# A one-layer streaming encoder step on one core: tail turns moved, keys in two places, norms moved, squares in PSUM

## The reference

```python
h = rmsnorm(x, g_mix); proj = h @ w_in            # 1024 x 2560
a, gate, q, k, v = split(proj)                    # 512 each, 8 heads x 64
u = a * sigmoid(gate)
c = causal_dwconv(concat(past_conv, u), w_dw) + b_dw      # 31 taps a channel
c = silu(layernorm(c, g_cn, b_cn)) @ w_pw
q, k = rmsnorm per head; z = q.k/8, masked s < t
A[t,s] = sigmoid(z[t,s]) * prod_{s<j<t} (1 - sigmoid(z[t,j]))
o = A @ v
x = x + concat(c, o) @ w_out
x = x + relu(rmsnorm(x, g_ff) @ w_ff1)**2 @ w_ff2         # 4096 wide
```

## Time and profile before

| | |
|---|---|
| time, median of 3 | 3094.45 us (3091.27 to 3097.13) |
| the profiled execution | 3089.33 us, span 3087.5 us |
| busy | PE 2774.3 us (90%), DVE 1719.1 (56%), ACT 1008.2 (33%), POOL 753.0 (24%) |
| DMA | 616.19 MB, mean 200 GB/s |
| mean granted PE clock | 0.955 of full |

### The profile page before, as it was taken

The page is one execution under the profiler, slowest core; times in us unless marked ns, Lnnn a source line. Parts: engine busy times, 40 slices in busy tenths (PEclk is TensorE's granted clock), DMA queues, the critical chain, the costliest instruction groups (busy, mean ns, idle before and its releaser), DMA issues. The chain is left out here.

```text
span 3087.5 us, 37298 instructions
## 1 busy us (share of the span) xinstructions
PE 2774.3 (90%) x13936; PEld 2304.8 (75%) x13936; DVE 1719.1 (56%) x2617; ACT 1008.2 (33%) x2017; POOL 753.0 (24%) x622
## 2 busy tenths in 40 slices
PE   5679766798999989899999989899999999999999
PEld 4556555677778777778888878677778777888887
DVE  4686663655667246646777436753778862322222
ACT  4222432234555112124554221222555540211110
POOL 4431332444555102102222002200333320000000
PEclk9789878899999999899999999899999999999999
DMA  8277457567676855656554653674444347344342
GB/s 308 102 259 268 145 183 256 218 242 259 235 258 230 309 202 190 216 180 245 185 181 161 251 205 134 201 253 180 152 161 158 110 163 287 154 173 155 149 179 86
DMA packets 262047, 616.19 MB, mean 200 GB/s; under 512 B 23217, under 2 KB 159409, under 8 KB 213741
## 3 DMA queue, kind: packets, MB, share of 16 engines
q1 hardware_dynamic: 261869, 613.80, 55.8%
HBM read 444.79 MB, written 168.94 MB: 199 GB/s over the span
## 5 line engine op out<-in xcount | busy, mean ns | idle before, releaser
L1081 POOL TENSOR_TENSOR beta<-beta,stay 128x512 f32<-128x512 f32 (+3 forms) x328 | 324.5, 992 | 769.6 <-DVE stay L1722 769.6
L1862 PE MATMUL ps<-h2T_hi,w_s 128*128 128x512 f32 (+1 forms) x1280 | 467.5, 365 | 15.3 <-ACT kqT L1252 7.9
L2152 PE MATMUL ps<-w_s,hid_hi 128*128 128x512 f32 (+1 forms) x1088 | 437.0, 402 | 20.9 <-DVE hid_lo L1796 20.9
L1863 PE MATMUL ps<-h2T_lo,w_s 128*128 128x512 f32 (+1 forms) x1280 | 455.4, 356 | 0.0
L1864 PE MATMUL ps<-h2T_hi,w_s 128*128 128x512 f32 (+1 forms) x1280 | 455.3, 356 | 0.0
L2153 PE MATMUL ps<-w_s,hid_lo 128*128 128x512 f32 (+1 forms) x1088 | 426.1, 392 | 0.0
L2154 PE MATMUL ps<-w_s,hid_hi 128*128 128x512 f32 (+1 forms) x1088 | 425.8, 391 | 0.0
L1352 ACT ACTIVATE stay<-ps 128x512 f32<-128x512 f32 (+3 forms) x328 | 173.5, 529 | 495.9 <-DVE ps L1710 272.5
L994 POOL TENSOR_TENSOR w_s<-w_raw,w_s 128x1024 fp32r<-128x1024 f32 x94 | 244.7, 2623 | 327.1 <-ACT w_s L1138 327.1
L1791 DVE TENSOR_TENSOR resid<-ps,resid 128x512 f32<-128x512 f32 x256 | 176.1, 688 | 258.2 <-PE ps L2154 257.7
L1526 DVE SCALAR_TENSOR_TENSOR cacc<-uT,vecs,cacc 128x512 f32<-128x512 f32 (+1 forms) x360 | 288.5, 857 | 1.5
(11 more groups left out here) (195 smaller groups left out, 4963.0 us busy)
## 6 DMA issues: line engine op xcount, KB each, us to landing
w_s<-w_scratch SPq DMA_DIRECT2D x282, 1024.0 KB, 7.7
w_scratch<-w_s SPq DMA_DIRECT2D x94, 1024.0 KB, 8.0
w_raw<-in_w_ff SPq DMA_DIRECT2D x64, 512.0 KB, 5.0
a_k<-k_scratch SPq DMA_DIRECT2D x80, 256.0 KB, 4.1
a_v<-v_scratch SPq DMA_DIRECT2D x80, 256.0 KB, 3.9
a_q<-q_scratch SPq DMA_DIRECT2D x64, 256.0 KB, 4.7
w_raw<-in_w_in SPq DMA_DIRECT2D x20, 512.0 KB, 7.4
mix_scratch<-ohl SPq DMA_DIRECT2D x66, 128.0 KB, 2.8
```

Source lines behind the costliest of these rows:

```text
L1081: nc.gpsimd.tensor_tensor(v[0:q.r, 0:n], v[0:q.r, 0:n], stay[q.z % 3][0:q.r, 1:n + 1], ALU.mult).then_inc(s_a, 1)
L1862: nc.tensor.matmul(out, w[0], x[0], start=start, stop=False)
L1863: nc.tensor.matmul(out, w[0], x[1], start=False, stop=False)
L2152: nc.tensor.matmul(o, hid_hi[x][:, k, q0:q0 + r], wh[:, c0:c0 + BANK], start=k == 0, stop=False)
```

## The change

- Tail of `kvq(c)`, c = 0, 2, 3: the last two query tiles are turned, copied and stored in slots of the next stage (`TAIL_TURN`: slots 2 and 6 of `front()`, 1 and 3 of a window). The turns use banks 3 and 7, the events the three banks 4 to 6, and PE waits for the last gate (`ag_u`) ahead of the first event.
- Chunk 0's attention: heads take turns in two places for keys and values, so SP loads two heads ahead; `att_past(0)` is 58 in place of 78, so the 41 steps lie in slots 31 to 57 and the loads for `out(0)` are issued at slot 58. Chunk 1's taps in `front()` are moved: 8 in slots 31 to 57 in place of 24, and 47 from slot 58 on in place of 31.
- Chunk 1's input norm goes from `ag(0)` to `kvq(0)` (squares and roots to the second half of `ag(0)`, scaling to its end, turns after events 0 to 3, in banks 1 and 2). The loads of `xsecond` move from the start into `ag(0)`.
- `xin` has four buffers; tiles 2 and 3 are loaded at the end of the window ahead of `out`.
- Feed forward: ACT writes Relu and then Square into the bank itself; DVE's product and `hid_f` go. ff2 results 0 and 1 are interleaved, so that the matmuls of k = 3 come after 18 others in place of 9.
- The transposes for the conv state in the last window go from slot 1 to slot 6.

```diff
 def att_past(c):
-    return 78 if c == 0 else 116
+    return 58 if c == 0 else 116
...
-        hid_f = [place("hid_f0", [P, 4, CHUNK], F32, o_hid + 8 * KIB),
-                 place("hid_f1", [P, 4, TMAX], F32, o_a + 8 * KIB + 4 * TMAX * 4)]
...
-        xin = place("xin", [P, 2, D], F32, o_a + 36 * KIB)
+        xin = [place(f"xin{i}", [P, D], F32, o) for i, o in enumerate(
+            (o_a + 36 * KIB, o_a + 40 * KIB, o_hid + 8 * KIB, o_hid + 12 * KIB))]
...
+        def norm_bank(which, c):
+            return 4 if which else 1 if c == 1 else 6
+
+        def kv_place(c, head):
+
+            return head % 2 * BANK if c == 0 else 0
...
+        KVQ_BANK, KVQ_BANKS, TURNED = 4, 3, (3, 7)
+
+        TAIL_TURN = [(2, 6), (1, 3), (1, 3), (1, 3)]
+
+        def tail_turn(c, slot, later):
+
+            n = len(kvq_events(c))
+            return [n - 2 + k for k in range(2) if c != 1 and TAIL_TURN[c][k] + later == slot]
...
-                due = 0 if t < a else min(n, 5 * (t - a + 1) // 4) if t < 31 else n * 4 // 13 + (n - n * 4 // 13) * (t - 30) // 58
+                due = 0 if t < a else 5 * (t - a + 1) // 4 if t < 31 else 25 + (t - 30) // 3 if t < 58 else 34 + 3 * (t - 57) // 2
...
-                if i >= 2:
-                    sp.wait_ge(n_tp[0], 2 * (4 * c + i - 1))
-                sp.dma_start(xin[0:r, i % 2, :], src).then_inc(x_in[i % 2], 16)
+                if i >= 4:
+                    sp.wait_ge(n_tp[0], 2 * (4 * c + i - 3))
+                elif i >= 2:
+                    sp.wait_ge(f2_ps, 8 * FFE * (c - 1))
+                sp.dma_start(xin[i % 4][0:r, :], src).then_inc(x_in[i % 4], 16)
...
+                    if c == 0 and a < 4:
+                        sp.dma_start(xsecond[:, a, :], x_prompt[0, CHUNK + P * a:CHUNK + P * (a + 1), :]).then_inc(xf_in[a], 16)
...
             def load_keys(c, head, s):
-                sp.dma_start(a_k[:, s * BANK:(s + 1) * BANK].bitcast(F32),
+                at = s * BANK + kv_place(c, head)
...
+                if c == 0:
+                    load_keys(0, 1, 0)
+                    load_values(0, 1, 0)
...
+                    following = q.head + (1 if c else 2)
+                    if q.p == 1 and q.ends and following < NH:
                         sp.wait_ge(z_ps, q.z + 1)
-                        load_keys(c, q.head + 1, q.a0 // BANK)
+                        load_keys(c, following, q.a0 // BANK)
...
+                        for late in tail_turn(n, s, 2):
+                            store_turned(n, late)
...
+                if 0 < n < NC - 1:
+                    for i in range(2, 4):
+                        load_x(n + 1, i)
...
-                    if c == 0 and a == 0:
-                        for i in range(4):
-                            norm_squares(0, 1, i)
-                        act.wait_ge(cache_out, 32)
-                    if c == 0 and a in (3, 5, 7):
-                        norm_hi(0, 1, a // 2 - 1)
+                    if c == 0 and a >= 4:
+                        norm_squares(0, 1, a - 4)
...
-                        nc.scalar.activation(hid_f[x][:, j, s0:s0 + w], bank, ACT.Relu).then_inc(f_rel, 1)
+                        nc.scalar.activation(bank, bank, ACT.Relu).then_inc(f_rel, 1)
+                        act.wait_ge(f_rel, f + 1)
+                        nc.scalar.activation(bank, bank, ACT.Square).then_inc(f_sq, 1)
...
-                    if c == 0:
-                        if m < CB - 1:
-                            norm_scale(0, 1, m)
-                        if m == CB - 2:
-                            norm_scale(0, 1, 3)
                     if m < CB - 1:
                         if m == 0:
                             dve.wait_ge(vec_ok, 2)
                             dve.wait_ge(cache_out, 32)
                         dve.wait_ge(ag_u, 4 * c + (m + 1) * ns)
                         convolve(c, range(EARLY * m, EARLY * (m + 1)))
-                    if c == 0 and m:
-                        norm_lo(0, 1, m - 1)
+                    if c == 0 and m == CB - 2:
+                        norm_scale(0, 1, 0)
                 if c == 0:
-                    norm_lo(0, 1, 3)
+                    for i in range(1, 4):
+                        norm_scale(0, 1, i)
...
+                    if c == 0 and 1 <= s <= 4:
+                        norm_lo(0, 1, s - 1)
...
-                        dve.wait_ge(f_rel, f + 1)
-                        nc.vector.scalar_tensor_tensor(out=bank, in0=bank, scalar=0.0, in1=hid_f[x][:, j, s0:s0 + w],
-                                                       op0=ALU.max, op1=ALU.mult).then_inc(f_sq, 1)
-                    if pos >= 8:
-                        ev = pos - 8
+                    results = [] if pos < 9 else [0, 1] if pos == 9 else [pos - 8]
+                    for ev in results:
...
+            def turn_both(c, s):
+                sec, i, m = kvq_events(c)[s]
+                if sec != "v":
+                    for q in range(2):
+                        if m:
+                            pe.wait_ge(kqT_ok, 2 * (8 * c + m) + q - 1)
+                        turn_packed(c, s, q, TURNED[q])
+
             def kvq(c):
                 evs = kvq_events(c)
                 if c:
                     pe.wait_ge(n_lo[1], 2 * (4 * (c - 1) + len(tiles(c - 1))))
-                else:
-                    pe.wait_ge(n_lo[0], 16)
-                for s in range(len(evs) + 2):
-                    if s < len(evs):
-                        if s >= 4:
-                            pe.wait_ge(kvq_cp, 12 * c + s - 3)
-                        project(c, s, 4 + s % 4, range(KD))
+                for s in range(len(evs)):
+                    if s >= KVQ_BANKS:
+                        pe.wait_ge(kvq_cp, 12 * c + s - KVQ_BANKS + 1)
+                    if s == 0:
+                        pe.wait_ge(ag_u, 4 * c + 4 * len(splits(c)))
+                    project(c, s, KVQ_BANK + s % KVQ_BANKS, range(KD))
+                    if c == 0 and s < 4:
+                        norm_turn(0, 1, s)
                     if s >= 2:
-                        sec, i, m = evs[s - 2]
-                        if sec != "v":
-                            for q in range(2):
-                                if m:
-                                    pe.wait_ge(kqT_ok, 2 * (8 * c + m) + q - 1)
-                                elif q == 0:
-                                    pe.wait_ge(ag_u, 4 * c + 4 * len(splits(c)))
-                                turn_packed(c, s - 2, q, q)
+                        turn_both(c, s - 2)
...
-                pe.wait_ge(kqT_ok, 16)
-                pe.wait_ge(kvq_cp, 12)
                 for t in range(FRONT):
+                    for late in tail_turn(0, t, 0):
+                        turn_both(0, late)
+                    if t == ln0(0):
+                        pe.wait_ge(kqT_ok, 16)
+                        pe.wait_ge(kvq_cp, 12)
...
+            def second(c, e, ev, ks):
+
+                i, hf = ev // 2, ev % 2
+                q0, r = tiles(c)[i]
+                nt, ns, x = len(tiles(c)), len(splits(c)), c // (NC - 1)
+                if 0 in ks:
+                    if ev < 3:
+                        pe.wait_ge(f_lo, 4 * FFE * c + 4 * ns * (e + 1) - (2 - ev))
+                    else:
+                        pe.wait_ge(f2_add, 8 * FFE * c + 2 * nt * e + ev - 2)
+                o = ps[0:r, ff_bank(c, e, 4 * ns + ev), :]
+                for k in ks:
+                    if ev < 2:
+                        pe.wait_ge(f_lo, 4 * FFE * c + 4 * ns * e + (k + 1) * ns)
+                    wh, wl = slab("f2", c, 4 * e + k)
+                    c0 = hf * BANK
+                    nc.tensor.matmul(o, hid_hi[x][:, k, q0:q0 + r], wh[:, c0:c0 + BANK], start=k == 0, stop=False)
+                    nc.tensor.matmul(o, hid_lo[x][:, k, q0:q0 + r], wh[:, c0:c0 + BANK], start=False, stop=False)
+                    ins = nc.tensor.matmul(o, hid_hi[x][:, k, q0:q0 + r], wl[:, c0:c0 + BANK], start=False, stop=k == 3)
+                if 3 in ks:
+                    ins.then_inc(f2_ps, 1)
...
+                        for late in tail_turn(n, s, 0):
+                            turn_both(n, late)
+                        if s == TAIL_TURN[n][1] + 2:
+                            pe.wait_ge(kqT_ok, 2 * (8 * n + 2 * len(tiles(n))))
+                            pe.wait_ge(kvq_cp, 12 * n + 3 * len(tiles(n)))
...
+                        if ev == 0:
+                            second(c, e, 0, range(3))
+                            second(c, e, 1, range(1))
+                        elif ev == 1:
+                            second(c, e, 1, range(1, 3))
+                            second(c, e, 0, range(3, 4))
+                            second(c, e, 1, range(3, 4))
                         else:
-                            pe.wait_ge(f2_add, 8 * FFE * c + 2 * nt * e + ev - 2)
-                        o = ps[0:r, ff_bank(c, e, 4 * ns + ev), :]
-                        for k in range(4):
```

(9 more changed lines are left out.)

93 lines of the change are left out of this document (47 added, 46 removed).

## The result

The changed kernel takes 3022.20 us (median of 4 runs, 3019.73 to 3026.41); before, beside it, 3094.52 (3091.27 to 3097.13). The ratio is 0.9773, 95% interval 0.9761 to 0.9784: 70 us faster by the ratio, 72 by the medians. The forecast was 2981, range 2940 to 3035. So the sign and the range held, and the time is 41 us above the forecast. The profiled execution took 3021.44 us, with a span of 3019.6: 68 of the 112 us in the sum came.

What follows compares the result with a forecast made beforehand. PE was taken as the bound in the feed-forward windows, so only its idle time and slow clock could be won. Terms 27 + 28 + 10 + 15 + 15 + 17 = 112 us off 3089 gave 2977, predicted median 2981, range 2940 to 3035.

Steps and rivals of the forecast that it cites:

- A: Start up to chunk 0's layer norm: chunk 1's norm leaves ag(0), last turns covered by front() slots; -27 us.
- The page weighed in A: Skill page: DVE with one SBUF input isn't blocked by GpSimd, so eight norm_lo cost 5.5 us, not 17.
- B: Attention in front(), slots 31 to 79: key waits go, steps take 2.7 us; -28 us.
- C: End of front(): mix loads issued at slot 58 shorten the 17.41 us wait before out(0); -10 us.
- D: Tails of kvq(2) and kvq(3): waits for the last turned tiles go; -15 us.
- E: Input tiles of chunks 2 and 3: third tile's waits of 9.64 and 5.68 us shrink by earlier loads; -15 us.
- F: Feed forward: most of the 20.9 us of waits for hid_lo go; -17 us.
- R1: Start and front() held by transfers and DVE: gain 45 to 80 us, about 3025 us; chance 0.16.
- the forecast's own: Band of the main forecast for the whole kernel: -80 to -140 us; chance 0.64.
- R3: ACT becomes the bound of the windows, slower, about 3205 us; chance 0.04 with anything slower.

Runs made afterwards that it cites:

- `pw_late`: Changed kernel with the two casts of the pw slabs 5 slots later on ACT, behind the squares of chunk 0's layer norm: 3024.01 us, ratio 0.9780.
- `half_reload`: Changed kernel with work left out: reloads of chunk 1's 20 projection slabs fetch only the high half, 0.5 MB in place of 1 MB: 3010.69 us, ratio 0.9733.
- `tails_x`: Changed kernel with last two turned tiles of chunks 2 and 3 turned at slot 0, their later input tiles loaded late as before: 3039.40 us, ratio 0.9820.
- `ff_order`: Changed kernel with Square kept on ACT and only the interleaving of the first two ff2 results taken back: 3042.72 us, ratio 0.9839.
- `ff_old`: Changed kernel with the old feed forward: Relu into SBUF, product on DVE, 9 matmuls ahead of group 3's first user: 3042.62 us, ratio 0.9842.
- `mix_later`: Changed kernel with chunk 0's 4 MB of mix loads issued at slot 71 of front() in place of slot 58: 3016.42 us, ratio 0.9754.
- `old_pace`: Changed kernel with chunk 0's attention over slots 31 to 77, mix loads at slot 78 and the old tap schedule; two key places kept: 3010.91 us, ratio 0.9734.
- `taps_even`: Changed kernel with mix loads at slot 71 and the old, even tap schedule in front(); attention stays packed: 3014.73 us, ratio 0.9757.

## Why the prediction was right and where it was wrong

- **A, forecast 27, measured 10.** Up to 96 us it came as worked out: event 0 at 95.4 (forecast 96), waits of 9.8 and 3.3 to 3.8 us. Three steps failed behind it. The first is "these three events take 3.3 + 1.1 + 1.1 + 5.4 = 11 us": the waits were right, but the turns and matmuls were priced at the full clock, and events 2 and 3 took 14.4 and 14.0 us at a granted clock of 0.74. At event 5 (163.2 before, 153.3 now) 9.9 us were left, where 16 were forecast. The second is "PE's last waits of this stage, 12 us of those of L1933 in the earlier trace rows, are covered by slots of `front()`, where PE meets DVE again at slot 10": it is not DVE that PE meets there. PE's first matmul of the layer norm came at 230.31 (245.95 before; the prediction read 248), a gain of 15.6: the slots covered 5.7 us and not 11. DVE's last tap ended at 226.6, 9 us ahead of before, and DVE stood idle. What came last was the copy and the store of the last turned tile, moved into `front()` with its turn; `pw_late` showed that its copy can come 9 us earlier for nothing, `half_reload` that the bytes beside it count. The third is that the norm itself was put at nothing: from its first matmul to pw it took 25.4 us before and takes 30.8 now, with the wait for that store in it. The forecast counted PE and DVE in this stretch and not its DMA, although the row for it could have been asked for: 0.64 is the mean over the 93 us of the earlier trace rows, and the last 22 of these read, in the kernel before:

```profile
200.00:222.00 22.00, 9.10 (x40) 7.36 (x40) 21.05 (x30) 6.06 (x12) 13.02 (x10) 0.82 1.00 357
```

- **The page weighed in A** held: `norm_lo`, one input in SBUF and one in PSUM, took 1.27 us for two beside POOL's gain product (DVE, at 112.14), 0.64 each. By the row of `packed` it would have been 2.1. `packed`, with both inputs in SBUF, took 1.35 us beside the same kind of POOL instruction (at 122.87), and taps with theirs in SBUF 1.98 each beside the splits (the four at 433.83). The Trainium skill (SBUF — State Buffer, Who interferes with whom) has it so. The term failed elsewhere.
- **B, forecast 28, and C, 10; measured 14.7 together.** The waits on keys are gone, and the attention of 41 steps runs from 287.0 to 399.8, 2.75 us a step (forecast 2.7). That the size fits is partly luck: 8.2 of these 112.8 us are the wait behind the `ohl` store, which no term had. The step that failed is "The 22 slots after them are 22 x 1.36 = 30 and six turns, 36 us". With the 3 us taken off B and C's rest of 17 the forecast comes to 56 us from there to `out(0)`; it took 78.6. These slots were priced by PE alone. They hold the v stores behind the mix loads, the four splits on POOL, the taps and the q tiles' chain. C's own wait did shrink (3.72, forecast 6 to 8), but what the 4 MB cost had moved ahead, to the v stores and the wait at 454.5. That the key places at the old pace bring 28.5 us, the size of B, is chance: B took that from a sum in which the attention was packed, and packing with mix loads and taps costs 13.8.
- **D and E, forecast 15 + 15.** Taking them back costs 15 to 20 us (`tails_x`), in which one wait of each tail is missing. Behind `out(0)` 42.9 us were won; less the 18.4 of the interleaving, at most 24.5 are left for both, so the pair was put at least 5 us too high. The waits themselves did as forecast: those of 9.64 and 5.68 us are both 1.54 now, though the second tile of chunk 2 waits 3.04 in place of 1.54. How the shortfall is shared between the two is open.
- **F, forecast 17, measured 20 (18 to 19 in the traces).** The size was right, and its parts as argued: interleaving carries it and the DVE product counts nothing. But it isn't made of the waits it was added up from: `hid_lo` keeps two waits of 12.6 us in sum and not 5, so 8 of the 20.9 are gone and not 17, while `ff_order` has 13.2 more than the changed kernel and `ff_old` 15.9. Attention's waits on `aT_lo` rose from 16.8 to 27.8, which `ff_old` (29.2) shows not to come from Square; the 10.9 more lie in `front()`, in the packed attention.
- **The rivals.** The 72 us of the medians lie in R1's band (45 to 80) and not in the forecast's own. R1 had the size: "A to C give a third, 22 us, and D to F stay at 47", 3025. Its cause was half right: transfers do hold A (`half_reload`) and part of the end of `front()` (`mix_later`), not `ag(0)`, where the slabs passed at a DMA share of 0.90 and 345 GB/s (38.4 to 95.4 us) without a wait of PE for one. R3 is out: in the windows PE waits 0.8 us for ACT's sigmoids.

What stays open: what makes the 20.7 us at the first late turn, of the splits on POOL, DVE's load and the store ahead; which of pace and mix loads makes `old_pace` faster than `taps_even`, and what the four out slabs' splits would cost ahead of slot 58 or in smaller pieces between the q tiles; neither was run. Nor is it known how much of the 12 us of `half_reload` lies behind pw for the reason that it does ahead of it.

## What to carry to other kernels

When a step is moved, price its store and the buffer that the store frees, by the DMA share of the stretch it lands in and not of the stage around it: a mean of 0.64 hid a stretch at 1.00. When work is packed to end early, price what was lying beside it on every engine; twenty slots that look empty on PE were DVE's, POOL's and the queue's. And to hide a chain of three instructions, put more matmuls in front of its first user: that was worth 20 us, while moving one instruction of the chain to another engine, which left the chain 0.13 us shorter, was worth nothing that could be told.

## What the runs showed of the hardware

- Relu and Square from a PSUM bank to the same bank take 511 and 507 ns in the mean on ACT, no more than Relu from PSUM to SBUF before (525).
- A store of 0.5 MB issued 4 us behind 4 MB of loads landed 11.2 us after its issue, the next one, issued at 427.05, in 5.5 (to 432.57). A store of 128 KB issued right behind 4 MB of loads (362.18) landed after 11.4 us, with a median of 2.5 over the run.
- SP was busy for 7.89 us with two issues in a stretch with a DMA share of 1.02 (`pw_late`, 220 to 229 us), where two of the same line took 1.87 at 213.57 (share 0.74), and everything behind them in its queue stood for that long.
